# Neighbourhood attention with scores split into two reduced-precision halves, two head pairs staged, and the pointwise bias added by VectorE

## What is computed

```python
# neighbourhood attention: 16 heads of width 64, four grid rows of 64
s_loc = einsum('bwhd,bawkhd->bhwak', q_r, k_win) + bias   # 4 x 16 neighbours
s_ctx = einsum('bwhd,bchd->bhwc', q_r, kc)                # 256 context keys
p = softmax(concatenate([s_loc, s_ctx], -1))
out = einsum(p_loc, v_win) + einsum(p_ctx, vc)
...
# the convolution branch beside it
y = layer_norm(depthwise_conv(glu(u)))
yc = (silu(y) @ conv_pw + conv_pw_b) * silu(gate)
```

## Time and profile before

| | us |
|---|---|
| median of 3 runs | 3490.7 |
| lowest, highest | 3485.49, 3494.09 |
| the profiled execution | 3488.28 |
| its span, first to last instruction | 3486.2 |

### The profile page before, as it was taken

How to read it: one execution, slowest core, us unless ns; L and a number is a source line. 1 busy time by engine, 2 the same in 40 slices (tenths; PEclk the granted TensorE clock), 3 DMA queues, 4 the chain that set the end, 5 groups by cost and what they waited for, 6 DMA issues and landing times.

```text
span 3486.2 us, 40825 instructions
## 1 busy us (share of the span) xinstructions
PE 3388.2 (97%) x15230; PEld 2724.6 (78%) x15230; DVE 2281.0 (65%) x4121; ACT 1547.3 (44%) x2894; POOL 45.0 (1%) x50
## 2 busy tenths in 40 slices
PE   9999999999998999999999999999999989999998
PEld 7888878888887888887887888888567766888666
DVE  6888887777765888888776335555464346645655
ACT  5444444456655544444555222222353344422454
POOL 0000000000000000000000000000100000000100
PEclk9999999999999999999999999999899999999899
DMA  7777777775546777777874333333103245534224
GB/s 263 257 260 256 250 266 240 261 244 173 154 158 197 256 258 258 262 257 259 265 265 165 93 91 96 98 97 97 52 1 121 74 139 146 169 97 119 102 70 160
DMA packets 285001, 613.77 MB, mean 176 GB/s; under 512 B 18882, under 2 KB 21506, under 8 KB 282884
## 3 DMA queue, kind: packets, MB, share of 16 engines
q1 hardware_dynamic: 280804, 596.26, 52.9%
q0 software_dynamic: 2048, 9.37, 0.8%
q10 hardware_dynamic: 1952, 5.54, 0.5%
HBM read 604.80 MB, written 6.29 MB: 175 GB/s over the span
## 4 chain that ended last, share of the span: by engine, by line
PE 80%; DVE 9%; DMA 6%; ACT 4%; issue 2%; ACTq 0%; SPq 0%; DVEq 0%
PE acc L401 24%; PE acc L403 23%; PE acc L402 23%; DMA raw<-ffn_w_gu 6%; DVE lo L396 3%; PE acc L2207 2%; PE acc L2181 2%; ACT hi L392 1%; DVE cgw L1151 1%; DVE mw L1153 1%; PE tp L2194 1%; PE tp L2158 1%; PE tp L1823 0%; DVE tm L1713 0%; DVE rn L1613 0%
## 5 line engine op out<-in xcount | busy, mean ns | idle before, releaser
L396 DVE TENSOR_TENSOR lo<-raw,hi 128x512 fp32r<-128x512 f32 x1808 | 1209.1, 689 | 931.3 <-ACT hi L392 923.8
L392 ACT ACTIVATE hi<-raw 128x512 fp32r<-128x512 f32 x1808 | 1116.6, 630 | 1581.1 <-PE acc L403 1296.6
L401 PE MATMUL acc<-hi,hT_hi 128*128 128x512 f32 x1760 | 702.8, 399 | 28.5 <-DVE hT_lo L1138 12.7
L401 PE MATMUL acc<-hi,h_hi 128*128 128x512 f32 x1696 | 674.9, 398 | 22.1 <-DVE lo L396 17.6
L402 PE MATMUL acc<-hi,hT_lo 128*128 128x512 f32 x1760 | 687.7, 391 | 0.0
L403 PE MATMUL acc<-lo,hT_hi 128*128 128x512 f32 x1760 | 687.6, 391 | 0.0
L403 PE MATMUL acc<-lo,h_hi 128*128 128x512 f32 x1696 | 663.0, 391 | 0.0
L402 PE MATMUL acc<-hi,h_lo 128*128 128x512 f32 x1696 | 662.3, 391 | 0.0
L401 PEld LDWEIGHTS acc<-hi,hT_hi 128*128 128x128 f32 x1760 | 331.2, 188 | 121.0 <-DVE hT_lo L1138 22.1
L401 PEld LDWEIGHTS acc<-hi,h_hi 128*128 128x128 f32 x1696 | 319.5, 188 | 102.4 <-DVE lo L396 32.1
L403 PEld LDWEIGHTS acc<-lo,hT_hi 128*128 128x128 f32 x1760 | 331.6, 188 | 70.5
(11 more groups left out here) (278 smaller groups left out, 2340.7 us busy)
## 6 DMA issues: line engine op xcount, KB each, us to landing
raw<-ffn_w_gu SPq DMA_DIRECT2D x352, 512.0 KB, 5.5
raw<-w_in SPq DMA_DIRECT2D x280, 512.0 KB, 3.8
mw<-wmt SPq DMA_DIRECT2D x192, 512.0 KB, 5.2
raw<-ffn_w_down SPq DMA_DIRECT2D x176, 512.0 KB, 5.3
raw<-w_out SPq DMA_DIRECT2D x96, 512.0 KB, 4.1
ball<-rpbx SPq DMA_DIRECT2D x8, 768.0 KB, 8.5
x_rest<-x POOLq DMA_DIRECT2D x2, 2048.0 KB, 9.9
x<-x_rest SPq DMA_DIRECT2D x2, 2048.0 KB, 7.7
```

Of the source, the lines that this page charges most:

```text
L392: act.activation(hi[:, g % RING, :], raw_piece(g), ACT.Copy).then_inc(S["hi_made"], 1)
L396: dve.tensor_tensor(lo[:, g % RING, :], raw_piece(g), hi[:, g % RING, :].bitcast(F32), ALU.subtract).then_inc(S["lo_made"], 1)
L401: pe.matmul(bank, act_hi, hi[:, slot, :], start=start, stop=False)
```

## The change

Four things are done together.

1. `T` is replaced by a rounded half and a rest, `Th` and `Tl`, two buffers of each. ACT writes `Th` (`hi_q`, `hi_k`), DVE writes `Tl` (`lo_q`, `lo_k`), and each score is three F32R matmuls in place of one F32 matmul. The pair is staged in step 1 of a lap and taken in steps 1 and 2. A pair's rope is done in step U of the lap ahead, two pairs ahead; pairs 0 and 1 are rotated before the first unit.
2. The mask is laid into the bias table on the host; its transfer and POOL's eight instructions go.
3. The pointwise bias is no matmul; `cpb` is fetched to all 128 rows, and DVE adds it in two halves and multiplies by the gate in two halves.
4. DVE writes a tile's `zb` ahead of the gate of the tile two before it, not behind it.

```diff
+        Th = [at(f"Th{k}", H + (4, 35)[k] * K1, [P, 2 * CH], F32R) for k in range(2)]
+        Tl = [at(f"Tl{k}", H + (31, 23)[k] * K1, [P, 2 * CH], F32R) for k in range(2)]
...
-                sp.dma_start(cpb[:], a["conv_pw_b_2"][ly:ly + 1, :]).then_inc(S["cf_in"], 16)
+                sp.dma_start(cpb[:], row_bc(a["conv_pw_b_2"][ly:ly + 1, :], CH)).then_inc(S["cf_in"], 16)
...
-                sp.dma_start(mask[:], a["mask"]).then_inc(S["na_in"], 16)
...
+                def hi_q(pair):
+                    act.wait_ge(S["cg_done"], cgs + 2 * pair + 1)
+                    act.activation(Th[pair % 2][:, 0:nt * P], cg[0][:, 0:nt * P], ACT.Copy,
+                                   scale=NA_D ** -0.5).then_inc(S["th_made"], 1)
+
+                def hi_k(pair):
+                    act.wait_ge(S["cg_done"], cgs + 2 * pair + 2)
+                    act.activation(Th[pair % 2][:, CH:2 * CH], cg[1][:], ACT.Copy).then_inc(S["th_made"], 1)
...
                 def step(lap, k, end):
-                    if k == 1 and end > U:
-                        stage_ctx(lap, 1)
+                    if k == U and lap < 6:
+                        stage_ctx(lap, 2)
                     if k + 1 < end:
                         na_exp(lap, k + 1)
-                    if k == U - 2 and end > U:
-                        take_k(lap, 1)
+                    if k == 1 and end > U:
+                        hi_q(lap + 1)
+                    if k == 2 and end > U:
+                        hi_k(lap + 1)
                     if k < end:
                         na_pt(lap, k)
...
+                def lo_k(pair, ly=ly):
+                    dve.wait_ge(S["th_made"], 16 * ly + 2 * pair + 2)
+                    dve.tensor_tensor(Tl[pair % 2][:, CH:2 * CH], cg[1][:], Th[pair % 2][:, CH:2 * CH].bitcast(F32),
+                                      ALU.subtract).then_inc(S["cg_taken"], 1)
...
                 def step(lap, k, end):
                     na_sum(lap, k - 1)
-                    if k == 1 and end > U:
-                        rope(lap, 1, 0)
+                    if k == U and lap < 6:
+                        rope(lap, 2, 0)
                     if k + 1 < end:
                         na_max(lap, k + 1)
-                    if k == U - 2 and end > U:
-                        take_q(lap, 1)
+                    if k == 2 and end > U:
+                        lo_q(lap + 1)
                     na_out(lap, k - 1)
-                    if k == 1 and end > U:
-                        rope(lap, 1, 1)
+                    if k == 2 and end > U:
+                        lo_k(lap + 1)
+                    if k == U and lap < 6:
+                        rope(lap, 2, 1)
...
-                    dve.tensor_tensor(gC[:, t], tp[t % 2][:], gC[:, t], ALU.mult).then_inc(S["yc_made"], 1)
+                    for k in range(2):
+                        cols = slice(k * L, (k + 1) * L)
+                        ins = dve.tensor_tensor(r2[k], tp[t % 2][:, cols], cpb[:, cols], ALU.add)
+                    link(ins)
+                    for k in range(2):
+                        cols = slice(k * L, (k + 1) * L)
+                        ins = dve.tensor_tensor(gC[:, t, cols], r2[k], gC[:, t, cols], ALU.mult)
+                    ins.then_inc(S["yc_made"], 1)
...
+                conv_gate(nt - 2)
+                lo_q(0)
+                lo_k(0)
                 conv_gate(nt - 1)
+                dve.wait_ge(S["yc_made"], (4 if ly else 0) + nt)
                 dve.wait_ge(S["gates_made"], ly + 1)
-                take_q(0, 0)
+                rope(0, 1, 0)
+                rope(0, 1, 1)
                 na_max(0, 0)
...
-                    pe.matmul(tp[t % 2][:], ones[0:1, :], cpb[:], start=False, stop=True).then_inc(S["pw_done"], 1)
...
+                        pe.matmul(dst, qh[r, qs], qh[r, ks], start=True, stop=False)
+                        pe.matmul(dst, ql[r, qs], qh[r, ks], start=False, stop=False)
+                        ins = pe.matmul(dst, qh[r, qs], ql[r, ks], start=False, stop=True)
...
-                    if k == U - 2 and end > U:
+                    if k == 1 and end > U:
                         staged(lap, 1)
...
-                for pair in range(NA_H // 2):
-                    bv = bias[:, 2 * pair:2 * pair + 2].rearrange("p h (r n) -> p (h r) n", n=GRID)
-                    pool.tensor_tensor(bv, bv, mask[:].unsqueeze(1).broadcast_to([P, 12, GRID]), ALU.add)\
-                        .then_inc(S["bias_ready"], 1)
```

## The result

| kernel | median, us | lowest to highest | runs |
|---|---|---|---|
| before | 3487.5 | 3481.6 to 3494.1 | 8 |
| after | 3515.2 | 3502.8 to 3530.1 | 8 |

The changed kernel takes 1.0085 times as long, with a 95% interval of 1.0066 to 1.0104. It is slower, where the forecast was 3481.5 and faster. The profiled execution took 3514.97, with a span of 3513.2 against 3486.2. That difference of 27.0 us can be read off the trace by stretches of the program. The marks are the start of the last projection matmul ahead of a stage, the stage's first turn, and the first transpose of the output projection behind its laps.

The account below looks back on a forecast made before the run. PE's own work was taken as some 92% of the attention laps, rope waits the rest. Stage 1 gains 11.5 us, stage 2 loses 2.3: 3490.7 - 9.2 = 3481.5, its own range 3477 to 3487, 8 in 10 for 3465 to 3520.

Parts of the forecast that it names:

- Scores: Attention scores: three F32R passes for one F32 matmul gain 0.17 us per score, making a full step 2.31.
- Start of stage 1: Up to stage 1's first turn: earlier `zb` and no bias matmul, 7.3 us gained, PE idle 5 us before it.
- Steps of stage 1: Stage 1 laps of 16.6 to 16.8 us, staging wait 1.5; gains 1.7 at low clock, 1.5 in six laps, 1.0 last.
- Start of stage 2: Stage 2's start: first turn 0.5 us later, but POOL's mask work goes and low steps gain; together 3.4 gained.
- Laps of stage 2: Stage 2: an added key wait of 1.6 us makes laps 12.85, 1.3 more; five lose 6.4, the last gains 0.7.
- The clock: PE's granted clock in both stages: stage 1's low stretch lasts as before, 23.5 us, and laps are counted at full clock.
- Rival 1: Slower: new lap waits of 1.3 to 1.6 us bring the clock down in laps, 3497 to 3527 us; chance 0.36.
- Rival 2: Faster: low-clock stretches at the stages' starts get shorter, 3471 us for one, 3461 for both; chance 0.17.
- Rival 3: Faster: the key chain in stage 2's laps does not bind, nothing is lost there, 3475 us; chance 0.05.

Follow-up runs that it names:

- waits_moved: Kernel after with both PE waits in a lap removed by order: high and low halves made in step 1, rope spread over the last three steps; 3441.4 us.
- keys_early: Kernel after with only the high and low halves moved to step 1 of the lap, the rope left in step U; 3477.8 us.
- start_only: Kernel before with mask laid into the bias, pointwise bias added by VectorE and gates one tile later, its laps unchanged; 3477.2 us.
- waits_filled: Kernel after with three matmuls on constants in each staging wait and each key wait of stage 2, nothing moved; 3462.0 us.
- f32_waits_moved: Kernel after with both lap waits removed by order and F32 scores instead of three F32R passes, no low halves; 3461.2 us.
- f32_longer_waits: Kernel after with F32 scores, no low halves, and waits lengthened by one doubled rope operation and the key copy in four quarters; 3557.5 us.
- start_filled: Kernel after with nine matmuls on constants in PE's idle before a stage's first turn, lap waits left in; 3504.9 us.

## Why the prediction was wrong

Step by step, as the prediction put it:

- **Scores.** Right. A full step is 2.32 (forecast 2.31). Behind the first, the passes start 0.23 apart at 512 columns and 0.12 at 256, and a step with a context score is 2.33, so the 0.70 taken for its six passes fits. Score to turn 0.89.
- **Start of stage 1.** Direction right, size too small: 11.1 gained to the first turn, not 7.3. The rest is the low stretch in before's first pointwise matmuls, which the forecast left in place. That it is missing in after is not the change's doing alone: the profiles of `waits_moved` and `keys_early`, with the same start, have one and take 35.3 us instead of 32.4 to the first turn, a gain of 8. PE idled 4.7 us before the first turn (forecast 5). `start_only`, which has the starts of both stages, gains 10.3 us of the whole.
- **Steps of stage 1.** The lap at 1.00 was 16.36 (forecast 16.6 to 16.8), the staging wait 1.37 (1.5).
- **Start of stage 2.** 0.3 later (0.5). POOL no longer stands beside the rope.
- **Laps of stage 2.** The wait that the change adds is there, where it was forecast: 1.52 (1.6), released by `Tl`. The lap is 12.87 with the clock kept up (12.85).
- **The clock.** This is the step that failed. Its price was put at nothing: the forecast took the low stretch of stage 1 "as it did" and all laps behind it at 1.00, on the ground that before's laps held it. It carried that over to a kernel whose laps have other waits. Before's waits at the staging were 0.93 by its sum and are 0.87 in the trace; the new ones are 1.2 to 1.5, and the runs show that this is enough: 0.7 to 1.05 seldom or never brought the clock down, 1.18 to 1.5 did so in every kernel that had them at full clock, though not at every such wait, and with both gone or filled no fall began in a lap. From the 0.50 stretches in after, 42 of its us in stage 2 and some 14 in stage 1 (144.6 against the 130.7 of `waits_filled`) are the clock's: in stage 2 the lap waits suffice for nearly all of it, in stage 1 most is the stretch behind the start. That stretch too was taken over from before, 23.5 us long behind 1.4 us of idle, while the forecast's own sum put 5 us of idle there; it was 34. What makes it short in one kernel or run and long in another stays open. Without its low stretches after would stand near 3462, 20 below the forecast, since before's own low stretches of 23.5 and 34.0 us shrink too.

**Rival 1** named this mechanism, and its page of the Trainium skill (TensorE: Matmul & The Clock Gate, A second HAM failure mode: psum-queue depth-cycling) says it in kind: many short idle stretches make the clock go to and fro, and the trace agrees, with three falls in stage 1 at 1.37 us of idle. It had 0.36 and should have had most of the chance. The reason held against it, that the new waits stand between full-height transposes and values where before's 1.4 did not, is what the runs refute: full-height work around the wait did not protect; the clock held in the laps where the wait was filled, taken away, or (mostly) 1.05 us or less. Its prices were off in both directions. A low lap of stage 2 takes 19.51 (18.6 forecast), and nearly all were low, not two; in stage 1 a fall in the laps costs 1.4 us (17.76 against 16.36), not 10, because there the clock came back each time within the lap.

**Rival 2** came true in some of the experiments, not in the change: in `waits_moved` the first low stretch is 5.6 us, in `f32_waits_moved`, just as free of lap waits, 35. In after it was 34 and 44 us, longer than before. Rival 3 fell: the key chain binds.

## What to carry to other kernels

When a change adds a wait to PE inside a loop that ran at full clock, price it twice: its own length, and the loop at half clock; here waits that made a lap 1.3 us longer by themselves cost about 40 us in one stage by the clock. Read the longest wait in the loop, not the busy share: after's PE was 97% busy. First move such a wait away by order, which gives back its length too (3441 here, against 3462 with the waits filled). Where an idle of PE can't be moved away, as the one before the first turn, put a few matmuls on constants into a free bank there: in these kernels a fill inside a wait cost no time. And trace more than one execution where the times of a kernel scatter: a single profile can show the rare one.

## What the hardware showed that I had not expected

- Either of two waits in a lap suffices to bring the clock down, and taking away one gains 6 to 37 us where both give 74.
- An idle of 4.4 to 4.75 us before a stage's first turn brought the clock down each time, for 5 us in some kernels and for 113 in one, with PE busy all the while; where it was filled, the stage began at 1.00.
- The clock need not come back when PE is busy again. In `keys_early` PE was busy for 57.8 of 58.5 us at 0.50, in `f32_longer_waits` for 113.9 of 115.3 in stage 2. The same kernels also show low stretches of 7 us. What ends one was not found.
- The falls have a rhythm. In after's stage 1 (and in `start_filled`) every second staging brought one, with the same 1.37 us of idle at each.
- A low clock hides its cause: at 0.50 the staging wait of after's stage 2 shrinks to 0.24 and the key wait to 0.97, so the rows of the low stretch show less idle than the laps at 1.00 that began it.
- Kernels that touch the low clock scatter (after 0.8%, `f32_longer_waits` 2% between its lowest and highest run), the one that never does lies within 0.1%.
